# Grouped attention with the values as the stationary operand, sums divided through a diagonal, and retention in another order behind it

## The reference

```python
attn_x = _attend(qa, concat([ka_c, ka]), concat([va_c, va]))     # softmax(q k^T / 8) v, 8 heads of 64
...
u = einsum('bhnjk,bhnjv,hj->bhnkv', kc, vc, zeta)                # per chunk of 128, both directions
s = g_chunk * s + u_n                                            # a scan over the chunks
out = intra + cross                                              # decayed scores x v, plus q x state
ret_x = _ret_output(out, gn_g, gn_b, gr)                         # group norm per head, silu gate
x_new = x + gt1 * (concat([attn_x, ret_x], -1) @ w_out)
h2 = _modulate(_rmsnorm(x_new, norm2_g), sh2, sc2)
x_new = x_new + gt2 * _hier_moe(h2, ...)                         # top group of 4, 2 of its 8 experts
```

## Time and profile before

| | us |
|---|---|
| time, median of 3 runs | 1810.71 |
| lowest and highest of them | 1804.58, 1817.32 |
| the profiled execution's own time | 1808.62 |
| its span | 1806.8 |
| PE busy, share of the span | 1598.4, 88% |
| DVE busy | 909.5, 50% |
| ACT busy | 531.7, 29% |
| POOL busy | 182.9, 10% |
| mean granted clock of TensorE | 0.942 |

### The profile page before, as it was taken

One profiled execution on the slowest core, in us unless ns is written; L12 is line 12 of the kernel. 1 busy time (PEld: TensorE's weight loads), 2 busy tenths in 40 slices (PEclk: granted clock), 3 DMA queues, 4 the chain that ended last, 5 costly groups with the idle time before them and its releaser, 6 DMA issues.

```text
span 1806.8 us, 22679 instructions
## 1 busy us (share of the span) xinstructions
PE 1598.4 (88%) x8416; PEld 1150.1 (64%) x8416; DVE 909.5 (50%) x1563; ACT 531.7 (29%) x828; POOL 182.9 (10%) x263
## 2 busy tenths in 40 slices
PE   6699999798899989998999899797999898989880
PEld 6588888577688868787788788676434333333330
DVE  3876537566457656576698576664111111111115
ACT  3312222467243254543522554212101010101011
POOL 2000010033010000001220130110000000000002
PEclk9899999889999999998999989895999999999995
DMA  9222354101232310314362012226899999999984
GB/s 369 77 110 96 139 193 161 53 13 42 94 128 106 129 50 22 129 48 169 130 226 100 1 47 94 96 86 259 350 423 423 423 423 422 423 423 422 423 351 145
DMA packets 55794, 353.06 MB, mean 195 GB/s; under 512 B 7408, under 2 KB 7664, under 8 KB 18720
## 3 DMA queue, kind: packets, MB, share of 16 engines
q1 hardware_dynamic: 43056, 306.88, 42.4%
q0 software_dynamic: 12656, 45.07, 6.7%
HBM read 332.26 MB, written 23.59 MB: 197 GB/s over the span
## 4 chain that ended last, share of the span: by engine, by line
PE 60%; DMA 16%; DVE 14%; ACT 3%; issue 3%; SPq 3%; POOL 0%; DVEq 0%; POOLq 0%; ACTq 0%
PE ps L2035 11%; PE ps L2037 10%; PE ps L2036 10%; DMA early<-in_experts 10%; PE ps L2473 6%; PE ps L2221 5%; PE ps L2089 4%; DMA raw<-in_experts 3%; PE ps L2494 3%; PE ps L2454 2%; SPq L636 2%; PE ps L2245 2%; ACT p L918 1%; PE ps L2014 1%; PE ps L2238 1%
## 5 line engine op out<-in xcount | busy, mean ns | idle before, releaser
L2035 PE MATMUL ps<-whi,xth 128*128 128x512 f32 (+1 forms) x768 | 303.8, 396 | 9.1 <-DVE xtl L1606 5.5
L2036 PE MATMUL ps<-wlo,xth 128*128 128x512 f32 (+1 forms) x768 | 300.2, 391 | 0.0
L2037 PE MATMUL ps<-whi,xtl 128*128 128x512 f32 (+1 forms) x768 | 300.1, 391 | 0.0
L1935 DVE TENSOR_TENSOR hid<-hid,ps 128x256 f32<-128x256 f32 x33 | 13.9, 422 | 371.8 <-ACT hid L1162 371.8
L2035 PEld LDWEIGHTS ps<-whi,xth 128*128 128x128 f32 x768 | 147.6, 192 | 39.0 <-DVE xtl L1606 5.8
L2037 PEld LDWEIGHTS ps<-whi,xtl 128*128 128x128 f32 x768 | 147.1, 192 | 30.2
L2036 PEld LDWEIGHTS ps<-wlo,xth 128*128 128x128 f32 x768 | 147.8, 192 | 28.9
L2473 PE MATMUL ps<-early,xe_t 128*64 128x512 f32 x624 | 142.3, 596 | 13.8 <-DMA early<-in_experts 12.6
L1211 DVE TENSOR_TENSOR wlo<-raw,whi 128x2048 fp32r<-128x2048 f32 (+3 forms) x52 | 108.7, 2091 | 68.9 <-ACT whi L847 63.4
L847 ACT ACTIVATE whi<-raw 128x2048 fp32r<-128x2048 f32 (+2 forms) x46 | 85.5, 1858 | 121.8 <-DMA raw<-in_even 34.1
L2473 PE MATMUL ps<-raw,xe_t 128*64 128x512 f32 x432 | 101.3, 601 | 19.7 <-DMA raw<-in_experts 16.7
(11 more groups left out here) (430 smaller groups left out, 2830.7 us busy)
## 6 DMA issues: line engine op xcount, KB each, us to landing
early<-in_experts SPq DMA_DIRECT2D x129, 1024.0 KB, 26.1
raw<-in_experts SPq DMA_DIRECT2D x54, 1024.0 KB, 26.4
raw<-in_ada SPq DMA_DIRECT2D x40, 1024.0 KB, 6.2
ring<-in_experts SPq DMA_DIRECT2D x15, 1024.0 KB, 27.6
raw<-in_even SPq DMA_DIRECT2D x14, 1024.0 KB, 5.6
raw<-in_second SPq DMA_DIRECT2D x10, 1024.0 KB, 4.9
pair_dram<-tmp POOLq DMA_DIRECT2D x66, 128.0 KB, 5.9
early<-in_ada SPq DMA_DIRECT2D x8, 1024.0 KB, 18.3
```

The source lines that it names most:

```text
L2035: nc.tensor.matmul(v, a[0], b[0], start=first, stop=False)
L2036: nc.tensor.matmul(v, a[0], b[1], start=False, stop=False)
L2037: return nc.tensor.matmul(v, a[1], b[0], start=False, stop=last)
```

## The change

**Attention.** The values become the stationary operand (128 keys x 64 features of `kk`) and the transposed probabilities move (128 columns of `ptg`), so the output has features on the partitions and queries along the row. The two units of a pair go to the two row halves of one slot, hence to the two column halves of the array, and share the job `O(u + 1)`. The row sums now lie along the wrong axis for a division by partition. So DVE makes `share`, the identity times the reciprocal of each row's sum (two instructions of 128x128), PE multiplies it with a block of ones (job `O(u)`, two matmuls), ACT copies the outcome to `shares`, and one DVE instruction multiplies the output of both units with it (`o_f`). ACT rounds `o_f` straight into `xth` (`out_high`), DVE subtracts for `xtl` (`out_low`). `oa_rows`, its 16 transposes and their evacuations are gone; the rows of `w_out` are permuted on the host so that head h and h + 4 lie in one k-tile.

**Around it.** The projection `qr` is done before `gr`, and its rotation moves from the first four attention pairs to the place ahead of the attention's first transposes. POOL's scalings then follow each other without a wait for it. In retention, ACT copies RU to `gains` in SBUF and DVE scans from there; the order becomes RU0, rk0, RU1, rk1, RS, qw, and the weighted scores lie in the middle of the scan. RO waits for the end of the scan (`s_state`). Of the output projection's first half, two row tiles' first four k-tiles (the attention part) are done ahead of the mix transposes. Several buffers are placed elsewhere.

```diff
+    chunk("second", "qr", 4, lat)
     chunk("second", "gr", 3, lat)
-    chunk("second", "qr", 4, lat)
...
         plan.job("turn", "rk", j)
     for j in range(2):
+        plan.job("RS", j)
+    for j in range(2):
         plan.job("turn", "qw", j)
-    for j in range(2):
-        plan.job("RS", j)
     plan.job("gate", 2, 0)
     for m in range(LT):
         plan.job("RO", m)
-    for j in range(MIXES):
-        plan.job("mix", "second", j)
-    chunk("sout", "o", 0, lat)
+    chunk("sout", "o", 0, lat, ahead={4: [("mix", "second", j) for j in range(2)]})
...
+        share = at("share", xt_base, 45 * KB, [P, 2, P])
+        shares = at("shares", xt_base, 46 * KB, [P, 2, P])
+        o_f = at("o_f", xt_base, 47 * KB, [P, 2, P])
+        ptg = at("ptg", g_base, 0, [P, 2, TOK])
...
+            pool.wait_ge(s_kn, 2 * LT)
             for i in range(2):
                 faded(qw[:, :, :, 64 * i:64 * i + 64], qr[:], 4 + i).then_inc(s_wr, 1)
             pool.wait_ge(s_gnl, 16)
-            evacuated(pool, "second", "gr", NT - 1)
...
+            def out_high(u):
+                m, h = gqa_unit(u)
+                evacuated(act, "O", "gqa", u + 1)
+                at_ = slice(CTX + P * m, CTX + P * m + P)
+                own.free(nc.scalar.activation(xth[:, h, at_], o_f[:, u // 2 % 2, :], ACT.Copy), s_oh)
             for u in range(0, S_UNITS, 2):
                 for n in (u, u + 1):
                     v = filled(act, "T", "gqa", n)
                     if u >= 2:
-                        filled(act, "O", "gqa", n - 2)
+                        filled(act, "O", "gqa", u - 1)
                     own.free(nc.scalar.activation(ptg[:, n % 2, :], v[:, 0:TOK], ACT.Copy), ev("T", "gqa", n))
+                if u >= 2:
+                    out_high(u - 2)
+                v = filled(act, "O", "gqa", u)
+                if u >= 4:
+                    evacuated(act, "O", "gqa", u - 3)
+                own.free(nc.scalar.activation(shares[:, u // 2 % 2, :], v[:, TOK:TOK + P], ACT.Copy), ev("O", "gqa", u))
                 if u + 2 < S_UNITS:
                     exps("gqa", u + 2, pg, s_nbg)
                     exps("gqa", u + 3, pg, s_nbg)
                 if u == 6:
-                    act.wait_ge(s_arg, 2)
+                    act.wait_ge(s_arg, 3)
                     own.free(nc.scalar.activation(near[:], near[:], ACT.Exp), s_fade)
-            u = filled(act, "RU", 0)
-            own.free(nc.scalar.activation(state[halves[1], LT - 1, :], u[halves[1], 0:512], ACT.Copy), s_back)
+            out_high(S_UNITS - 2)
             for j in range(2):
+                v = filled(act, "RU", j).rearrange("p (k n) -> p k n", k=2)
+                own.free(nc.scalar.activation(gains[:, j], v, ACT.Copy), ev("RU", j))
                 v = filled(act, "turn", "rk", j).rearrange("p (k n) -> p k n", k=2)
...
+            for m in range(CT, NT):
+                evacuated(dve, "second", "qr", m)
+                spin(qr[:, m - CT, :], 4, m - CT, tmp[:, 0, 0:256], s_kn)
...
+            def sharing(u):
+                evacuated(dve, "S", "gqa", u)
+                evacuated(dve, "S", "gqa", u + 1)
+                st = soft[:, u % 4:u % 4 + 2, :]
+                own(nc.vector.reciprocal(st[:, :, 3:4], st[:, :, 2:3]))
+                if u >= 2:
+                    filled(dve, "O", "gqa", u - 2)
+                for n in range(2):
+                    own.free(nc.vector.tensor_scalar(share[:, n, :], ident[:], st[:, n, 3:4], None, ALU.mult), s_share)
+            def out_low(u):
+                m, h = gqa_unit(u)
+                dve.wait_ge(s_oh, u // 2 + 1)
+                at_ = slice(CTX + P * m, CTX + P * m + P)
+                own.free(nc.vector.tensor_tensor(xtl[:, h, at_], o_f[:, u // 2 % 2, :], xth[:, h, at_].bitcast(F32),
+                                                 ALU.subtract), s_ol)
             maximum("gqa", 0, s_nbg)
             maximum("gqa", 1, s_nbg)
+            sharing(0)
             for i in range(S_UNITS // 2):
                 u = 2 * i
-                for n in (u, u + 1):
-                    if n + 2 < S_UNITS:
-                        maximum("gqa", n + 2, s_nbg)
-                for n in (u, u + 1):
-                    m, h = gqa_unit(n)
-                    scaled_out("gqa", n, oa_rows[:, m, 64 * h:64 * h + 64], 64, TOK)
-                if i < 4:
-                    evacuated(dve, "second", "qr", CT + i)
-                    spin(qr[:, i, :], 4, i, tmp[:, 0, 0:256], s_qn)
-                elif i < 8:
+                for n in (u + 2, u + 3):
+                    if n < S_UNITS:
+                        maximum("gqa", n, s_nbg)
+                if i:
+                    out_low(u - 2)
+                v = filled(dve, "O", "gqa", u + 1)
+                evacuated(dve, "O", "gqa", u)
+                own(nc.vector.tensor_tensor(o_f[:, i % 2, :], v[:, TOK:TOK + P], shares[:, i % 2, :], ALU.mult),
+                    ev("O", "gqa", u + 1))
+                if u + 2 < S_UNITS:
+                    sharing(u + 2)
+                if 4 <= i < 8:
                     for n in range(2):
                         low_part(("sout", "o", (i - 4) // 2), 2 * (i % 2) + n, 4)
-                else:
+                elif i >= 8:
                     for n in range(2):
                         add_part(2, 8 + (i - 8) // 4, 2 * (i % 4) + n)
                 if i == 1:
                     near_powers()
                 if i == 12:
                     ada(2, 8)
...
+                for n in range(LT):
+                    evacuated(dve, "RU", n // 2)
+                    gain = gains[:, n // 2, n % 2, :]
+                    if n == 0:
+                        for half_, to in ((halves[0], 0), (halves[1], LT - 1)):
+                            own.free(nc.vector.tensor_copy(state[half_, to, :], gain[half_]))
+                    else:
+                        for h in range(R_HEADS):
+                            at_ = slice(P * h, P * h + P)
+                            for half_, to, of in ((halves[0], n, n - 1), (halves[1], LT - 1 - n, LT - n)):
+                                own.free(nc.vector.scalar_tensor_tensor(state[half_, to, at_], state[half_, of, at_],
+                                                                        fade[half_, 6, h:h + 1], gain[half_, at_],
+                                                                        ALU.mult, ALU.add), s_state)
                     own.wait()
+                    if n == 1:
+                        dve.wait_ge(s_fade, 3)
+                        weighted_scores(0)
+                        weighted_scores(1)
...
+            gqa_scores(0)
+            for u in range(0, S_UNITS, 2):
+                for w in (u, u + 1):
+                    evacuated(pe, "S", "gqa", w)
+                    turn(("T", "gqa", w), [pg[:, w % 3, P * a:P * a + P] for a in range(NT)], [P * a for a in range(NT)])
+                if u + 2 < S_UNITS:
+                    gqa_scores(u + 2)
+                v = begin("O", "gqa", u)
+                pe.wait_ge(s_share, u + 2)
+                for i in range(2):
+                    mm = nc.tensor.matmul(v[halves[i], TOK:TOK + P], half[:, 1:2].broadcast_to([P, 64]), share[:, i, :],
+                                          start=True, stop=True)
+                end(mm, "O", "gqa", u)
+                v = begin("O", "gqa", u + 1)
+                for a in range(NT):
+                    for i in range(2):
+                        mm = nc.tensor.matmul(v[halves[i], TOK:TOK + P], kk[:, a, P + 64 * i:P + 64 * i + 64],
+                                              ptg[:, i, P * a:P * a + P], start=a == 0, stop=a == NT - 1)
+                end(mm, "O", "gqa", u + 1)
+                if u == 24:
+                    ada(2, 8)
...
+            w = [parts("sout", "o", h) for h in range(2)]
+            early_tiles = [CT, CT + 1]
+            v = {}
+            def out_rows(m, kts):
+                for kt in kts:
+                    wk = tuple(x[:, kt % 4, :] for x in w[kt // 4])
+                    mm = three(v[m][:, 0:512], xt(kt, slice(P * m, P * m + P)), wk, kt == 0, kt == KT - 1)
+                if kt == KT - 1:
+                    end(mm, "sout", "o", m)
+            for m in early_tiles:
+                v[m] = begin("sout", "o", m)
+                out_rows(m, range(4))
+            two = [begin("mix", "second", j) for j in range(2)]
             for m in range(LT):
                 pe.wait_ge(s_ret, R_HEADS * (m + 1))
                 for kt in range(4):
                     mm = nc.tensor.transpose(two[kt // 2][:, SEQ * (kt % 2) + P * m:SEQ * (kt % 2) + P * m + P],
                                              or_rows[:, m, P * kt:P * kt + P], ident[:])
                     if m == LT - 1 and kt % 2:
-                        end(mm, "mix", "second", 2 + kt // 2)
-            evacuated(pe, "mix", "second", MIXES - 1)
+                        end(mm, "mix", "second", kt // 2)
+            evacuated(pe, "mix", "second", 1)
```

(9 more changed lines are left out.)

129 lines of the change are left out of this document (58 added, 71 removed).

## The result

The changed kernel takes 1797.84 us (median of 6 runs, 1795.30 to 1800.47) against 1808.77 us of the kernel before (6 runs): a ratio of 0.9929, 95% interval 0.9905 to 0.9953. Timed again later beside other kernels it was 0.9900 (0.9874 to 0.9927). So it is 0.7 to 1.0% faster, and the 1797.84 us lie 2.8 us over the 1795 of the forecast. But the 15 us of the forecast were not all there, and the output projection, which was to give 5 us, gave nothing.

The account below looks back on a forecast made before the run. PE bounds the attention; behind it DVE (scan, group norm), then PE (output projection). Gains 8.7 + 1.3 + 5.0 = 15.0 us from 1808.6 give 1793.6; between two ways of counting, 1795, range 1782 to 1812.

Parts of the forecast that it names:

- The matmuls of a pair: Attention, O on PE: 24 instructions at 53 ns, 1.28 us; PE's own work of a pair 4.12 instead of 5.45.
- Who is late next: Attention pairs: a loop around the maxima sets the period, 5.15 us, or 5.2 to 5.3 with side work.
- POOL's hold: Start of the attention: POOL's 18.8 us in one stretch holds DVE; the fourth maximum 4.6 us later.
- The steps with a stall: Attention, fourth to last maximum: twelve steps in 68.3 us instead of 80.3, with i = 12 at 10.3.
- case A: First attention pairs: POOL holds `share` as well as `out_low`; fourth maximum at 1033.2 instead of 1028.60, 4.6 lost.
- The rotation of `qr`: Ahead of the attention: 7.84 us fit into DVE's 8.94 us wait for ACT, costing nothing; cover 1.1 us.
- Retention: RU to RO: RO 2.8 us sooner, but its first row tile at half clock; 1.3 won (0.5 to 2.8).
- Output projection: 24 of 96 matmuls go into PE's 5.17 us idle time ahead of the mix; 5.0 won (3 to 5.5).
- the sum of the terms: Whole kernel: attention 8.7, retention 1.3 and output projection 5.0 us won, together 15.0.
- The clock: Rival, attention pairs: PE's gaps bring half clock; three to five pairs 1803 to 1809 us (0.12), most pairs 0.06.
- DVE held longer: Rival, attention pairs: POOL holds or dearer DVE instructions make the period 5.6, 1800 to 1806 us; 0.24 with non-overlapping halves.
- halves that don't overlap: Rival, attention: O stays at 2.8, the pair at 5.66 us, total 1802; chance 0.24 with DVE held longer.

Follow-up runs that it names:

- the other profile of the kernel before: Kernel before with only the `h_rows` loads issued earlier, behind RO; run once: 1803.94 us beside 1804.42 of the kernel before.
- the tripled gate: Changed kernel with the eight products of gate(2, 0) done three times over; run once: 1795.77 us beside 1804.42 of the kernel before.
- The four kernels of the small table: Changed kernel, `h_rows` transfer late or early, with or without 24 products ahead; last norm to sout o's end: late 29.0, 27.9; early 22.95, 28.5 us.
- five edits of the stalls next to it: Changed kernel with early `h_rows` loads, `ada(2, 8)` first, POOL in pieces, gate tripled, decay powers behind the attention: 1780.40 us, 0.9821 to the kernel before.
- the slots: Changed kernel with sout o's third and fourth row tile in the mix transposes' PSUM slots, `h_rows` loads late: 1791.47 us, 0.9874 to the kernel before.
- the early transfers with nothing ahead: Changed kernel with early `h_rows` loads and no output-projection products ahead of the mix; run once: 1796.36 us beside 1809.75 of the kernel before.

## Why the prediction was right in its number and wrong in a term

**The matmuls of a pair** (O at 53 ns, 1.28 us): 1.48 us in the timeline, the last one's end included. The nearest row, RU, was the right one. PE's own work of a pair was forecast at 4.12 us; the windows have PE busy for 4.68 (5.47 before), so it is idle for 0.64 us and not for 1. Nothing hung on this, since PE no longer sets the pair.

**Who is late next** (a loop around the maxima of 5.15, and 5.2 to 5.3 with side work): measured 5.25 and 5.33, in the very chain that was worked out. For the twelve steps 68.3 us were forecast; from the fourth to the last maximum (1035.64 to 1103.30) it was 67.7. Of the 12.6 us that this is less than the 80.3 before, 9.8 are the two long steps of the earlier trace rows (11.25 and 9.10 against 5.3), the one with POOL's hold and the one at half clock behind it; the cheaper matmuls are the small part. This gain is in part chance: in the other profile of the kernel before, the same twelve steps took 72.6 us, and the loss lay ahead of them (the fourth maximum 25.2 us after the first scores instead of 20.5).

**The steps with a stall.** i = 12 was forecast at 10.3 and took 9.2: its transposes still ran at full clock after the wait, only the scores did not. In the second profile of the changed kernel it took 10.5, so how the clock falls there differs from execution to execution. The last O was 0.9 us nearer to the last maximum instead of 1.3.

**POOL's hold** (case A, 4.6 us lost at the start): the fourth maximum came 24.5 us after the first scores instead of 20.5, a loss of 4.0 (23.2 and a loss of 2.7 in the second profile). `share` was held, as in case A. Cutting POOL's work and moving it showed that POOL causes it.

**The rotation of `qr`**: costs at most 0.3 us, ahead of the stretch of the table. DVE reached its low part at 1008.88, when ACT had just finished `ka_h`; the forecast cover of 1.1 us had shrunk, because a weight transfer ahead of it came later.

**Retention**: RO starts 2.8 us sooner, as worked out; that it fits to the tenth is luck, as the other profile of the kernel before shows (22.3 us from RU to RO instead of 20.9). The half clock behind PE's 3.74 us of idling was forecast for the first row tile (1.5 us) and lasted 5.3 us, half way into the second: 2.0. The experiment with the tripled gate confirms the cause.

**Output projection**: this is the step that failed. "I take 5.0" rested on counting the 24 products that leave the stage, with DVE's modulation parts as the only thing that could be late. What was not followed is the slot: with two row tiles begun ahead of the mix jobs, the third takes the slot of the first and waits for its evacuation, and that stands behind the wait for `h_rows` on DVE, 4.65 us long in the kernel before already and harmless there. The wait and the half clock behind it took 6 us (4.5 in the second profile), about as much as the 5 that the products ahead bring. The four kernels of the small table show both numbers.

So the stages gave 9.5 us in these two profiles (8.5 to 11.2 over both pairs) instead of 15.0. The experts' first transfer came at 1205.64 us and not at 1197: 5.5 us from the sum and 3.0 from the later start. The timed difference is larger (10.9 between the medians, 12.8 by the ratio, 18 by the second ratio); these differ among each other by what the kernel before scatters, 1804 to 1821 us over all runs; its slower executions had the lower mean clock (0.946 at 1805.82 us, 0.933 at 1820.82). That 1795 was so near is thus in part luck: the sum of the terms was 3.8 to 6.5 us too high, and the scatter made up for it.

**The rivals.** The clock did not fall in steady pairs: 1.00 over ten of them, with a gap ahead of the transposes in each, 1.39 us once and 0.45 to 0.54 else. The rule of the Trainium skill ("TensorE: Matmul & The Clock Gate", "A second HAM failure mode: psum-queue depth-cycling") that frequent small gaps between groups of matmuls can make the clock swing was not borne out in this stage. DVE held longer, or halves that don't overlap, were not seen either.

## What to carry to other kernels

When work is moved ahead of a join, follow the buffer slots as well as the work: an early start holds a slot, and the next job may inherit a wait that was harmless. Look through the profile of before for long idle times on engines that nobody waits for (here 4.65 us on DVE for a transfer), and ask of each who would wait for it once the bound engine gets faster. A faster inner step shows its worth only when the stalls around it go: here PE saved 0.8 us of busy time in each pair (5.47 to 4.68) and the pair became 0.1 to 0.2 us shorter, while five edits of the stalls next to it gave 15.1 us more.

## What the runs showed of the hardware

Twenty-four matmuls with 64 stationary and 128 moving columns took 1.48 us when they went in turn to the two column halves and 2.40 us half after half; with 128 stationary and 64 moving columns it was 2.89. The order within one group decides much, and even half after half the new form is faster.

A DVE instruction that takes 0.29 us elsewhere took 4.48 while POOL multiplied 128x2048 elements in SBUF. With POOL's work in pieces of 0.6 and 1.2 us a pair of shares took 0.98 to 1.60 us instead of the 0.48 that it takes when POOL is idle; POOL's own three scalings then took 14.6 us instead of 12.8.

PE kept full clock through the gaps of the steady pairs, 0.45 to 0.54 us and once 1.39. Behind gaps of 2.0 to 3.7 us it often ran at half clock, but not always and not always at once. Behind the gap of 2.8 us at i = 12 the transposes of the changed kernel were still at full clock (1.50 us for twelve) and the scores were not; in three other profiles with the same gap (the slots, the tripled gate, and the early transfers with nothing ahead) the clock of that step was 1.00 throughout and the step took 8.2 us. Behind the same gap of 2.1 us RU ran at 0.78 in the changed kernel and at 1.00 with POOL in pieces.
